# Additions to x ahead of the next column pair's operand sums, and three plain units of each column pair with their lo half by an adding DMA

## The reference, cut to what matters

```
for l in range(DEPTH):                       # DEPTH = 2
    h = rmsnorm(x, norm1_g[l])
    proj = h @ w_in[l]                       # 2048 x 4352, then attention: out_a, out_b, out_c
    x = x + concatenate([out_a, out_b, out_c]) @ w_out[l]
    h2 = rmsnorm(x, norm2_g[l])
    x = x + square(relu(h2 @ w_up[l])) @ w_down[l]     # 2048 x 8192, 8192 x 2048
```

## Time and profile before

| | us |
|---|---|
| median of 3 runs | 2052.64 (2052.55 to 2052.8) |
| the profiled execution | 2053.29 |
| its span in the trace | 2051.5 |

### The profile page before, as it was taken

How to read it: one execution, slowest core, us unless ns; L and a number is a source line. 1 busy time by engine, 2 the same in 40 slices (tenths; PEclk the granted TensorE clock), 3 DMA queues, 4 the chain that set the end, 5 groups by cost and what they waited for, 6 DMA issues and landing times.

```text
span 2051.5 us, 27000 instructions
## 1 busy us (share of the span) xinstructions
PE 2037.3 (99%) x10626; PEld 1705.7 (83%) x10626; DVE 1543.4 (75%) x1991; ACT 1064.3 (52%) x1388; POOL 192.2 (9%) x196
## 2 busy tenths in 40 slices
PE   9999999999999999999999999999999999999999
PEld 8887788887887887888888877888788878878887
DVE  7767566799779779867677775666996897798674
ACT  6557644455455445444455586444544554554442
POOL 6253100000000000001023531000000000000000
PEclk9999999999999999999999999999999999999999
DMA  9477966666657665766665678666666576667663
GB/s 301 133 228 189 236 182 183 184 187 212 187 174 213 198 188 182 216 187 193 185 175 146 212 203 219 195 178 191 184 213 188 173 219 192 185 187 214 185 195 123
DMA packets 182878, 396.66 MB, mean 193 GB/s; under 512 B 13674, under 2 KB 22352, under 8 KB 182752
## 3 DMA queue, kind: packets, MB, share of 16 engines
q1 hardware_dynamic: 178064, 379.52, 61.2%
q0 software_dynamic: 4512, 15.33, 4.0%
q10 hardware_dynamic: 176, 0.09, 0.0%
HBM read 377.95 MB, written 2.12 MB: 185 GB/s over the span
## 4 chain that ended last, share of the span: by engine, by line
PE 89%; DVE 9%; issue 1%; DMA 1%; ACT 1%; SPq 0%; ACTq 0%
PE psum L575 23%; PE psum L599 23%; PE psum L602 12%; PE psum L579 12%; PE psum L644 5%; DVE w_lo L1094 3%; PE psum L647 2%; DVE t_lo L1102 2%; PE psum L703 1%; PE psum L609 1%; PE psum L610 1%; PE psum L613 1%; PE psum L686 1%; PE psum L690 1%; PE psum L687 1%
## 5 line engine op out<-in xcount | busy, mean ns | idle before, releaser
L897 ACT CAST w_hi<-raw_ring 128x1024 fp32r<-128x1024 f32 (+1 forms) x720 | 744.2, 1041 | 818.2 <-PE psum L602 365.9
L1094 DVE TENSOR_TENSOR w_lo<-raw_ring,w_hi 128x1024 fp32r<-128x1024 f32 (+1 forms) x692 | 845.9, 1228 | 382.1 <-ACT w_hi L897 380.5
L599 PE MATMUL psum<-xt,w_hi 128*128 128x512 f32 x2048 | 513.4, 392 | 0.3 <-issue 0.3
L599 PEld LDWEIGHTS psum<-xt,w_hi 128*128 128x128 f32 x2048 | 368.7, 189 | 67.1 <-issue 0.7
L602 PEld LDWEIGHTS psum<-xt,w_lo 128*128 128x128 f32 x2048 | 279.4, 190 | 20.0
L602 PE MATMUL psum<-xt,w_lo 128*128 128x256 f32 x2048 | 285.5, 282 | 0.0
L575 PE MATMUL psum<-w_hi,xt 128*128 128x512 f32 (+1 forms) x1152 | 281.3, 386 | 0.0
L575 PEld LDWEIGHTS psum<-w_hi,xt 128*128 128x128 f32 x1152 | 202.4, 188 | 40.5 <-issue 2.7
L575 PE MATMUL psum<-w_hi,ht_hi 128*128 128x512 f32 x512 | 203.0, 397 | 0.0
L575 PE MATMUL psum<-w_hi,ht_lo 128*128 128x512 f32 x512 | 199.8, 390 | 0.0
L644 PE MATMUL psum<-w_hi,ht_hi 128*128 128x512 f32 x384 | 151.7, 395 | 8.4 <-DVE x L1145 7.0
(11 more groups left out here) (200 smaller groups left out, 2150.2 us busy)
## 6 DMA issues: line engine op xcount, KB each, us to landing
raw_ring<-in_w_up_dram SPq DMA_DIRECT2D x256, 512.0 KB, 4.0
raw_ring<-in_w_down_dram SPq DMA_DIRECT2D x256, 512.0 KB, 4.2
raw_ring<-in_w_in_dram SPq DMA_DIRECT2D x128, 512.0 KB, 4.7
raw_ring<-in_w_out_dram SPq DMA_DIRECT2D x64, 512.0 KB, 4.9
w_lo<-raw_ring POOLq DMA_DIRECT2D x28, 512.0 KB, 6.6
raw_ring<-in_w_in_dram SPq DMA_DIRECT2D x16, 256.0 KB, 2.8
x<-in_x_dram SPq DMA_DIRECT2D x8, 256.0 KB, 7.7
out_dram<-x SPq DMA_DIRECT2D x3, 512.0 KB, 2.8
```

The costliest lines, as they stand in the source:

```text
L599: pe.matmul(bank[:, f, :], w_hi[:, w, j, f * P:(f + 1) * P], both, start=kt == 0, stop=False, skip_group_check=True)
L897: act.copy(w_hi[:, u % AHEAD, :, 0:cols], raw_ring[:, u % RAWS, :, 0:cols]).then_inc(hi_ready, 1)
L1094: dve.tensor_tensor(w_lo[:, u % AHEAD, :, 0:cols], raw_ring[:, u % RAWS, :, 0:cols], w_hi[:, u % AHEAD, :, 0:cols].bitcast(F32), ALU.subtr ...
```

## The change

- `SUMMED_UNITS` gets the units m = 4, 8 and 12 of every column pair, 18 more a layer (36 in the kernel). They are plain units. ACT makes the negated copy, POOL starts the adding DMA, DVE makes no split for them, and PE and SP wait for the landing.
- `take_quarters` moves from step 14 to step 13 of each column pair: three additions stand ahead of `first_sums` for the next pair's units 2 and 3, the fourth directly behind those sums and ahead of the split of unit 1.
- `take_totals` moves behind the split of unit 3 of d = 1, ahead of `t_lo`.
- In the last seven products of each pair PE finishes the product for the fourth quarter bank, lo part included, before it begins the other two.
- In the first seven products of d = 1 PE does the "quarters" ahead of "own", and the wait for `totals_out` moves from the start of the group to the start of "own". `unit_done` for both units is given at the end of "own".

```diff
-SUMMED_UNITS = list(range(55, 83, 2))
+SUMMED_PAIR = (4, 8, 12)
+SUMMED_UNITS = list(range(55, 83, 2)) + [LOOP0 + LOOP_UNITS * i + 16 * d + m for i in range(LOOPS) for d in range(2) for m in SUMMED_PAIR]
...
             def load_pair(pl, u, turn, d, m):
-                sp.wait_ge(split_done, pl.at(VECTOR_SPLITS, vector_splits(u - RAWS + 1) + RAWS, LOOP_UNITS))
+                raw_is_free(pl, u)
...
-                if first and d == 1:
-                    pe.wait_ge(totals_out, pl.l * LOOPS + pl.i + 1)
+                swap = last or first and d == 1
...
                 def own():
+                    if first and d == 1:
+                        pe.wait_ge(totals_out, pl.l * LOOPS + pl.i + 1)
                     pe.wait_ge(hi_ready, pl.unit(s + 1))
...
-                if last:
+                if swap:
                     quarters()
                     own()
...
                 pe.wait_ge(t_hi_ready, number + 1)
+                if last:
+                    bank, of, t, _ = products.pop(0)
+                    mm = three(bank, of, [t_hi[:, t, :], t_lo[:, t, :]], False, lambda: pe.wait_ge(t_lo_ready, number + 1))
+                    mm.then_inc(pair_done, 1)
...
-            def split_lo(pl, u, cols=CW):
+            def split_lo(pl, u, cols=CW, then=None):
                 after = seven_at(pl, u + 1)
                 if after is not None and after[0] == 0:
                     first_sums(pl, u + 1)
+                if then is not None:
+                    then()
...
                 if seven is not None and seven[0] == 1:
+                    if pair_at(pl, u)[1:] == (1, 2 * SEVEN[0] + 1):
+                        take_totals(pl, pair_at(pl, u)[0])
                     dve.wait_ge(t_hi_ready, seven[1] + 1)
...
-                if part == "pair" and k == 2 * KPS - 2:
-                    take_quarters(pl, s, c)
-                if part == "pair" and c == 0 and k == 2 * KPS - 1:
-                    take_totals(pl)
-                if s < UNITS - 1 and more:
+                if part == "pair" and k == 2 * KPS - 3:
+                    take_quarters(pl, s, c, range(3))
+                    split_lo(pl, s + AHEAD, then=lambda: take_quarters(pl, s, c, [3]))
+                elif s < UNITS - 1 and more and not is_summed(pl, s + AHEAD):
                     split_lo(pl, s + AHEAD)
```

More of the change, by code:

```diff
@@ L169, in vector_splits @@
 def vector_splits(n):
-    return n - sum(u < n for u in SUMMED_UNITS)
+    layer, u = divmod(max(n, 0), UNITS)
+    return min(n, 0) + layer * VECTOR_SPLITS + u - sum(v < u for v in SUMMED_UNITS)
 def before(n, parity):
@@ L340, in lo_sum_of, with is_summed @@
         def lo_sum_of(pl, u):
-            n = SUMMED_UNITS.index(u)
-            return lo_summed[n % 2], 16 * pl.at(len(SUMMED_UNITS) // 2, n // 2 + 1)
+            layer, v = divmod(pl.unit(u), UNITS)
+            n = SUMMED_UNITS.index(v)
+            return lo_summed[n % 2], 16 * (layer * (len(SUMMED_UNITS) // 2) + n // 2 + 1)
+        def is_summed(pl, u):
+            return pl.unit(u) % UNITS in SUMMED_UNITS
         def mlp_steps(first, kinds):
@@ L456, in _, with raw_is_free, load @@
         def _(sp):
-            def load(pl, u, w, width, offset, cols):
-                if u - RAWS in SUMMED_UNITS:
+            def raw_is_free(pl, u):
+                if is_summed(pl, u - RAWS):
                     sp.wait_ge(*lo_sum_of(pl, u - RAWS))
                 else:
-                    sp.wait_ge(split_done, pl.at(VECTOR_SPLITS, vector_splits(u - RAWS + 1) + RAWS, LOOP_UNITS))
+                    sp.wait_ge(split_done, vector_splits(pl.unit(u - RAWS + 1)) + RAWS)
+            def load(pl, u, w, width, offset, cols):
+                raw_is_free(pl, u)
                 sp.dma_start(raw_ring[:, u % RAWS, :, 0:cols],
@@ L555, in unit_is_split @@
             def unit_is_split(pl, u):
-                if u in SUMMED_UNITS:
+                if is_summed(pl, u):
                     pe.wait_ge(*lo_sum_of(pl, u))
                 else:
-                    pe.wait_ge(split_done, pl.at(VECTOR_SPLITS, vector_splits(u + 1) + RAWS, LOOP_UNITS))
+                    pe.wait_ge(split_done, vector_splits(pl.unit(u + 1)) + RAWS)
             def rows_unit(pl, u, src, kts, chunk, first, last, cols):
@@ L664, in own @@
                 def own():
+                    if first and d == 1:
+                        pe.wait_ge(totals_out, pl.l * LOOPS + pl.i + 1)
                     pe.wait_ge(hi_ready, pl.unit(s + 1))
                     three(psum[:, 0, :], h_tile(a, 0), w_tile(s, 0), first, lambda: unit_is_split(pl, s))
-                    three(psum[:, 1, :], s_tile(0), w_tile(s, 1), first).then_inc(unit_done, 2 if last else 1)
+                    three(psum[:, 1, :], s_tile(0), w_tile(s, 1), first).then_inc(unit_done, 2 if swap else 1)
                 def quarters():
@@ L674, in quarters @@
                     mm = three(quarter(0, 1), s_tile(3), w_tile(s + 1, 1), False)
-                    mm.then_inc(pair_done if last else unit_done, 1)
-                if last:
+                    if last:
+                        mm.then_inc(pair_done, 1)
+                    elif not swap:
+                        mm.then_inc(unit_done, 1)
+                if swap:
                     quarters()
@@ L688, in seven_products @@
                 pe.wait_ge(t_lo_ready, number + 1)
-                for n, (bank, (a_hi, a_lo), t, start) in enumerate(products):
+                for bank, (a_hi, a_lo), t, start in products:
                     mm = pe.matmul(bank, a_hi, t_lo[:, t, :], start=False, stop=True, skip_group_check=True)
-                    if last and n == 0:
-                        mm.then_inc(pair_done, 1)
                 mm.then_inc(sevens_done, 1)
@@ L1135, in quarter_x, with take_quarters, take_totals @@
                 return x[:, r, (2 * d + h) * CW:(2 * d + h + 1) * CW]
-            def take_quarters(pl, s, d):
-                for n, (r, h) in enumerate([(1, 1), (0, 0), (0, 1), (1, 0)]):
+            def take_quarters(pl, s, d, which):
+                for n in which:
                     if n == 0:
-                        dve.wait_ge(unit_done, pl.unit(s + AHEAD))
+                        dve.wait_ge(unit_done, pl.unit(s + 1 + AHEAD))
                     else:
                         dve.wait_ge(pair_done, pl.at(LOOPS * 6, 3 * d + n, 6))
+                    r, h = [(1, 1), (0, 0), (0, 1), (1, 0)][n]
                     v = quarter_x(r, h, d)
                     dve.tensor_tensor(v, psum[:, 4 + n, :], v, ALU.add).then_inc(pair_out, 1)
-            def take_totals(pl):
-                dve.wait_ge(sevens_done, sevens_after(pl, 0))
-                if pl.i == 0:
+            def take_totals(pl, turn):
+                dve.wait_ge(sevens_done, pl.l * SEVENS + (2 * turn + 1) * len(SEVEN))
+                if turn == 0:
                     dve.tensor_copy(totals[:, :, :], psum[:, 0:4, :]).then_inc(totals_out, 1)
```

## The result

| | before | changed |
|---|---|---|
| median | 2052.66 (4 runs) | 2072.71 (4 runs, 2070.14 to 2073.79) |
| the profiled execution | 2053.29 | 2070.14 |
| its span | 2051.5 | 2068.3 |

The changed kernel is slower: the ratio is 1.0095, 95% interval 1.0082 to 1.0107, so 20 us of 2053. The profiled execution is the fastest of the four, so the trace shows 16.8 us of the 20. The ratios of the experiments leave out two executions with a lower granted clock, one of experiment 1 (3386.79 us) and one of the kernel before (2224.92 us).

What follows compares the result with a forecast made beforehand. PE was taken as the bound, busy 2037.3 of 2051.5 us. Border gain -11.4 plus landing stalls +23.7 gave +12.3 on 2053.3, so 2065.6, as a median 2065 us; range 2044 to 2084.

Steps and rivals of the forecast that it cites:

- -11.4 + 23.7: Whole kernel: 11.4 us won at six borders, 23.7 us lost to late landings in six turns; together +12.3.
- the forecast's own chain: Border, DVE's queue after the additions: totals out at 468.4, PE at "own" at 468.7, so 0.3 us of slack.
- part 2: DVE's splits: 36 of 1.14 us removed, 41 us, worth nothing on PE's path beyond part 1.
- part 1: Border from d = 0 to d = 1: reordering gains 1.9 of 2.0 us, 11.4 us for six borders.
- part 3: Adding DMAs in the pairs: late landings stall PE 3.95 us in a turn, 23.7 us in six.
- the 7.6: Estimated us from issue to landing of an adding DMA behind four loads, taken from 7.0 to 7.9.
- The cross-check by DMA share: Share 0.62 in the first pair comes near the projections' 0.81, where half of the landings took more than 6.6 us.
- The faster one: Rival: sums in time except the eighth unit of d = 0, 0.3 us late; 2042 us, chance 0.20.
- The fit of the Trainium skill: GpSimd-issued DMA takes about 2.0 us plus bytes over 436 GB/s, 3.2 us for 512 KB; every sum in time, 2041.
- The burst as cause: SP waits for a landing, then sends four loads 0.4 us apart, taking 8.0 us, delaying the next adding DMA.
- The border does not go away: Rival: totals come 0.9 us late or more at the border; +5.4 on the forecast, 2070 us, chance 0.05.

Runs made afterwards that it cites:

- experiment 1: Changed kernel with no adding DMAs in the pairs, so only the new border: 2051.74 us, ratio 0.9993 to the kernel before.
- experiments 5 and 6: Adding DMAs in the pairs only at unit 4 of d = 0 and unit 12 of d = 1: new border 2045.25 us, old border 2046.70 us.
- experiment 2: Kernel before plus the adding DMAs at units 4, 8 and 12 of each pair, with the old border places and order: 2067.42 us, ratio 1.0070.
- experiment 3: Changed kernel without the adding DMA at unit 8 of each pair: 2060.01 us, ratio 1.0039 to the kernel before.
- experiment 4: Changed kernel, but adding DMAs in the pairs read w_hi, so loads wait only for ACT's negated copy, not the landing: 2097.12 us, ratio 1.0211.
- experiment 5: Changed kernel, new border, with adding DMAs in the pairs only at unit 4 of d = 0 and unit 12 of d = 1: 2045.25 us, ratio 0.9963.

## Why the prediction was right

The prediction was 2065 (2044 to 2084), slower; measured 2072.7. Its sum was -11.4 + 23.7. The trace of the profiled execution gives -12.0 + 29, which is its 16.8 us. So both terms had the right cause, and the second was 5 us too small.

**The border.** Forecast 1.9 of 2.0 us, measured 2.0, at all six. But the text gave the reason badly: it worked out that DVE would lose little even at its old time, and did not carry that case on to `totals`. Experiment 1 shows what that leaves out, a wait of 1.2 us. It is the splits saved in d = 0, 1.0 us from a single one (experiments 5 and 6), together with PE's own lateness from the stalls of d = 0 (experiment 2), that pay for the border. With both in place the forecast's own chain was met: `totals` was out at 470.73, and PE began "own" at 471.07, 0.3 us of slack as worked out. So part 2's "worth nothing beyond part 1" was true in words and hid the one thing that part 3 was buying.

**The landings.** From PE's timeline, start to start, means of six turns:

| unit | forecast late, us | measured late, us (least to most) |
|---|---|---|
| d = 0, m = 4 | 0 | 0 |
| d = 0, m = 8 | 1.6 | 1.4 (1.2 to 1.8) |
| d = 0, m = 12 | 0.85 | 1.0 (0.1 to 1.6) |
| d = 1, m = 4 | 0 | 0.5 (0.3 to 0.8) |
| d = 1, m = 8 | 0.65 | 1.1 (0.2 to 1.5) |
| d = 1, m = 12 | 0.85 | 0.4 (0 to 0.7) |

That is 4.4 us in a turn, and 4 or 5 slow restarts of 0.11 make it 4.9; forecast 3.95. Each mechanism was found in the trace. For d = 0 ACT is late at unit 8, and unit 4's DMA runs nearly alone; SP sends its loads out in a burst behind the landing. Three groups of answers of the changed kernel (unit 4, unit 12 of d = 0, SP between them):

```profile
L1680 POOL DMA_DIRECT2D w_lo<-raw_ring x1: 869/869/869, 425.7 to 425.7; - x1
...
DMA to landing us min/median/max: 4.6/4.6/4.6
...
443.75 1.90 SPq L519 DMA_DIRECT2D raw_ring<-in_w_down_dram  x4
...
L1680 POOL DMA_DIRECT2D w_lo<-raw_ring x1: 869/869/869, 447.4 to 447.4; - x1
...
DMA to landing us min/median/max: 8.3/8.3/8.3
```

Four loads start between 443.75 and 445.3, and the adding DMA issued 3.6 us behind the first takes 8.3 where I had estimated 7.6. For unit 12 of d = 0 the six turns had 6.8 to 8.3, mean 7.6, and 12 of the first layer's 18 adding DMAs in the pairs landed 2.3 to 2.6 us behind the landing of the last load issued ahead of them, which bears out the way in which the 7.6 was estimated (2.5 to 3). The cross-check by DMA share came out less well: between 420.9 and 464.0 the share is 0.73, up from 0.62 but not 0.81. SP's waits on landings are 64, as forecast:

```profile
SPq L472 <- DMA w_lo<-raw_ring: 282.1, 40, 10.3
...
SPq L519 <- DMA w_lo<-raw_ring: 190.8, 24, 10.0
```

**What was mis-sized.** Unit 4 of d = 1 was taken at 5.9 us with 6.4 available: it took 6.7, with two loads issued 2.6 and 1.4 us ahead of it. Its cost is 0.5 + 0.1, 3.4 us in six turns. Unit 8 of d = 1 was taken at 7.1: it took 8.1 in four turns of six. And the restart of 0.11 behind a late landing, 3 us in all, was in no term. The remaining 2.6 us between the profiled execution and the median are not placed in any row; the runs of the changed kernel spread over 3.7 us and those of before over 0.3. Late landings, which differ from turn to turn, would do that, but no trace of a slower run shows it.

**The rivals.** The faster one failed at its own condition, stalls under 1.2 us in a turn. The fit of the Trainium skill, page "DMA: Bandwidth & Descriptors", section "Anatomy of one DMA" (by it an estimate of 3.2 us for 512 KB) was not met by any adding DMA here: the fastest in all eight traces took 4.5. The burst as cause was right for the units that have one, but it is not a cost alone: experiments 3 and 4 show long landings with no burst, behind one or two single loads issued 0.3 to 3.2 us before the adding DMA. "The border does not go away" was the rival that I gave 0.05. It is what happens with the splits left in place and PE on time (experiment 1).

## What to carry to other kernels

Before taking work off an engine that is not the bound, ask at which point its queue is late, and take just enough there: here one split saved in the first pair of a turn won 6 to 8 of 12 us at no cost, and three adding DMAs in every pair left nothing of the 12 but cost 29. A DMA that stands in for 1.2 us of an engine's work has its landing time in the chain, so count its slack from the engine that starts it, with the loads in flight, and remember that an in-order load queue waiting for the landing keeps that DMA alone and crowds the next. An engine that is made late somewhere has its later waits covered by that, so do not credit the cure with all of them. When a wait goes, follow the same queue to its next item before counting the gain.

## What the runs showed of the hardware

- An adding DMA of 512 KB within the on-chip memory, in the pairs: it landed in 4.5 to 5.9 us when the last load had been issued 3 us or more before; in 5.1 to 6.0 with loads issued 2.7 and 1.6 us ahead (experiment 5); in 6.3 to 7.9 with loads 2.6 and 1.4 us ahead (changed kernel, experiment 3); and in 6.6 to 8.3 behind a burst of four (changed kernel).
- Behind a wait of PE for the landing of its operand, the second matmul comes 0.11 us late (28 of 29 places in the changed kernel; 0.10 at the other).
- In experiment 4 half clock came with waits of PE of 2.2 to 3.5 us, eight times: pitch 0.43 instead of 0.227, for 34 us together. Three waits of 2.5 to 2.7 us in that run, and those of up to 2.7 us in experiment 3 and 1.8 us in the changed kernel, left the clock at 1.00.
